# Hybrid attention block: window and selected branch through one exponential, in a trail of four pairs

## The reference, cut to what matters

```
def compressed_attention(q, k, v, slopes):      # 127 blocks of keys, each from 32 positions
    s = q.k * dh ** -0.5 - slopes * dist;  p = masked_softmax(s, mask);  return p.v, p
def select_blocks(p_cmp, T):                    # importance of 64-key blocks, summed over a group
    _, idx = lax.top_k(score, n_sel)            # 16 of 32 blocks for each query
def selected_attention(q, k, v, idx, slopes):   # softmax over the keys of those blocks, dist >= 0
def window_attention(q, k, v, slopes):          # softmax over the last 512 keys
```

## Time and profile before

| | us |
|---|---|
| median of 3 runs (lowest, highest) | 1832.9 (1832.1, 1835.3) |
| profiled execution | 1828.8 |
| its span, slowest core | 1827.8 |
| spans of the 8 cores | 1820.5 to 1827.8 |
| granted TensorE clock, mean | 0.986 to 0.992 |

### The profile page before, as it was taken

One profiled execution on the slowest core, in us unless ns is written; L12 is line 12 of the kernel. 1 busy time (PEld: TensorE's weight loads), 2 busy tenths in 40 slices (PEclk: granted clock), 3 DMA queues, 4 the chain that ended last, 5 costly groups with the idle time before them and its releaser, 6 DMA issues.

```text
span 1827.8 us, 27598 instructions; the slowest of 8 cores (1820.5 to 1827.8 us)
## 1 busy us (share of the span) xinstructions
PE 1714.7 (94%) x9938; PEld 883.2 (48%) x10082; DVE 684.7 (37%) x1257; ACT 502.1 (27%) x834; POOL 81.5 (4%) x157
## 2 busy tenths in 40 slices
PE   4999999999787888998899999999999999999998
PEld 1374746554666663443344444444444444444444
DVE  2334132111676758213635152332415051432415
ACT  4151253232787854445510000000000000000000
POOL 4000000000000010000000000000000000000000
PEclk9999999999999999999999999999999999999999
DMA  9912368334502096525241634527081735436155
GB/s 147 168 17 46 71 115 139 70 63 82 98 2 49 3 200 122 138 50 89 54 85 31 108 59 80 94 45 124 15 138 18 121 48 91 82 57 113 26 93 185
DMA packets 39988, 152.53 MB, mean 83 GB/s; under 512 B 4080, under 2 KB 12848, under 8 KB 26544
## 3 DMA queue, kind: packets, MB, share of 16 engines
q0 software_dynamic: 21456, 126.00, 40.5%
q1 hardware_dynamic: 18400, 24.75, 5.0%
HBM read 265.92 MB, written 8.45 MB: 150 GB/s over the span
## 4 chain that ended last, share of the span: by engine, by line
PE 85%; DMA 4%; DVE 4%; ACT 3%; issue 3%; POOL 0%; DVEq 0%; ACTq 0%; POOLq 0%
PE psum L1252 17%; PE psum L1250 17%; PE psum L1270 16%; PE psum L457 15%; PE psum L1091 6%; PE psum L464 3%; PE psum L900 3%; PE psum L796 3%; DMA arena<-xk 2%; PE psum L1165 2%; PE psum L1216 1%; DMA arena<-wall 1%; ACT arena L903 1%; DMA arena<-memk 1%; PE psum L1052 1%
## 5 line engine op out<-in xcount | busy, mean ns | idle before, releaser
L1078 DVE TENSOR_TENSOR arena<-psum,arena 128x512 f32<-128x512 f32 x432 | 298.3, 691 | 136.9 <-PE psum L1091 64.7
L457 PE MATMUL psum<-arena 128*128 128x512 bf16 (+2 forms) x1600 | 312.4, 354 | 9.7 <-DMA arena<-wall 2.9
L1252 PE MATMUL psum<-arena 128*128 128x512 bf16 x1379 | 316.6, 379 | 1.5
L1250 PE MATMUL psum<-arena 128*128 128x512 bf16 x1379 | 316.4, 379 | 1.5
L1270 PE MATMUL psum<-arena 128*128 128x512 bf16 x1381 | 304.3, 379 | 1.4
L1257 ACT ACTIVATE arena<-psum 128x512 bf16<-128x512 f32 x88 | 52.5, 597 | 824.3 <-PE psum L1250 804.5
L1258 DVE TENSOR_TENSOR arena<-psum,arena 128x512 bf16<-128x512 f32 x88 | 60.9, 692 | 536.2 <-PE psum L1250 423.2
L457 PEld LDWEIGHTS psum<-arena 128*128 128x128 bf16 x1600 | 147.0, 99 | 166.3 <-issue 22.9
L1252 PEld LDWEIGHTS psum<-arena 128*128 128x128 bf16 x1408 | 137.8, 98 | 166.1
L1270 PEld LDWEIGHTS psum<-arena 128*128 128x128 bf16 x1408 | 137.8, 98 | 166.1
L1250 PEld LDWEIGHTS psum<-arena 128*128 128x128 bf16 x1408 | 137.7, 98 | 166.0
(11 more groups left out here) (131 smaller groups left out, 979.4 us busy)
## 6 DMA issues: line engine op xcount, KB each, us to landing
arena<-wall POOLq DMA_DIRECT2D x102, 1024.0 KB, 13.3
arena<-wall POOLq DMA_DIRECT2D x10, 864.0 KB, 11.0
arena<-xk POOLq DMA_DIRECT2D x32, 256.0 KB, 46.3
arena<-xo SPq DMA_DIRECT2D x32, 256.0 KB, 8.1
y<-arena SPq DMA_DIRECT2D x32, 256.0 KB, 2.7
arena<-selscr SPq DMA_DIRECT2D x4, 1024.0 KB, 7.8
arena<-arena SPq DMA_DIRECT2D x16, 144.0 KB, 7.7
arena<-cbf SPq DMA_DIRECT2D x1, 1032.8 KB, 6.9
```

The lines of the kernel that those rows point to most:

```text
L457: op(PE, lambda: nc.tensor.matmul(bank[psi][:, 0:n], lhsT=wt[:, kc, cc * 128:(cc + 1) * 128], rhs=rhs(kc), start=(kc == 0), stop=(kc == 15 ...
L1078: op(DVE, lambda: nc.vector.tensor_tensor(out=dst, in0=bank[psi][:, :], in1=dst, op=ALU.add), r=[bankb[psi]], w=[xrb[d][tc]])
L1250: op(PE, lambda: nc.tensor.matmul(bank[pg][:, :], lhsT=wgt[:, kc, cc * 128:(cc + 1) * 128], rhs=h3T[tc][kc // 4][:, kc % 4, :], start=(kc ...
L1252: op(PE, lambda: nc.tensor.matmul(bank[pu][:, :], lhsT=wut[:, kc, cc * 128:(cc + 1) * 128], rhs=h3T[tc][kc // 4][:, kc % 4, :], start=(kc ...
```

## The change

The diff, cut to what acts. `cmp_job`, `branch_jobs` and the tiles change names in places that are left out.

```diff
-        qnT = self.tile(A, "qnT", [128, NH, TQ], BF16)
+        CT = self.scope()
+        qnT = self.tile(CT, "qnT", [128, NH, TQ], BF16, hi=True)
...
-        NP_ = 8
-        Pt = [self.tile(AT, f"Pt{j}", [128, 512], BF16) for j in range(NP_)]
+        NP_ = 7
+        Pt = [self.tile(AT, f"Pt{j}", [128, 2, 512], BF16) for j in range(NP_)]
-        rot_S = Rot([0, 1, 6])
-        rot_O = Rot([2, 4])
-        rot_T = Rot([7])
-        oc1 = [self.tile(AT, f"oc1_{j}", [128, 4, 128], F32) for j in range(4)]
+        sring = {"p": 0}
+        opair = {"s": 4, "w": 6}
+        def s_pair():
+            p = (sring["p"] + 1) // 2 * 2 % 4
+            sring["p"] = (p + 2) % 4
+            return p
+        def s_one():
+            p = sring["p"]
+            sring["p"] = (p + 1) % 4
+            return p
+        def o_swap():
+            opair["s"], opair["w"] = opair["w"], opair["s"]
+        oc1 = [self.tile(AT, f"oc1_{j}", [128, 4, 128], F32) for j in range(8)]
...
+        M = self.tile(AT, "selM", [128, 16, 512], BF16)     # now behind HG.close()
-        catA = self.tile(CT, "catA", [128, 8, TQ], BF16, hi=True)
+        catA = qnT
+        catTb = qnTb + [[self.buf(f"catT{c}_{t}") for t in range(2)] for c in range(8)]
-        def run_jobs(jobs, L=5):
+        def run_jobs(jobs, L=4, D=2):
+            pjs = []
+            done = 0
+            for n in range(len(jobs) + L + 2):
                 if n < len(jobs):
+                    pjs.append(jobs[n][0]())
+                if 0 <= n - D < len(jobs) and jobs[n - D][2] is not None:
+                    jobs[n - D][2](pjs[n - D])
+                while done < len(jobs) and done <= n - L:
+                    if jobs[done][3] and done == n - L:
+                        break
+                    jobs[done][1](pjs[done])
+                    done += 1
...
+        def stream(g, h, tc, oc, ocbuf, at=None):
             qts = QT[tc * 4:tc * 4 + 4]
+            for dl in range(qts[3] + 1):
                 j0 = min(j for j in range(4) if qts[j] >= dl)
+                last = dl == qts[3]
+                parts = [1, 0] if dl <= 4 else [1]
+                def sc(dl=dl, j0=j0, parts=parts):
+                    si = s_pair() if len(parts) == 2 else s_one()
+                    n0 = j0 * 128
+                    for part in parts:
+                        bi = si + (1 - part if len(parts) == 2 else 0)
...                          # triangle and score matmuls into bank bi, as before
+                    if len(parts) == 2:
+                        src = psum[:, si * 512:(si + 2) * 512].rearrange("p (b n) -> p b n", b=2)[:, :, n0:512]
+                        op(ACT, lambda: nc.scalar.activation(out=Pt[pj][:, :, n0:512], in_=src, func=AF.Exp, bias=ba), r=[bankb[si], bankb[si + 1], pvb], w=[Ptb[pj]])
+                    else:
+                        op(ACT, ...)             # one bank, as before
+                def mask(pj, dl=dl, j0=j0): ...  # the same masks, as a function of their own
+                def pvf(pj, dl=dl, j0=j0, parts=parts, last=last):
+                    if dl == 0:
+                        o_swap()
+                        st["s"], st["w"] = opair["s"], opair["w"]
+                    for part in parts:
+                        b0 = st["s" if part else "w"]
+                        vs = g if part else 2 + g
+                        pv(pj, 1 - part, j0, b0, ..., NV, dl == 0, last if part else dl == 4)
+                    if dl == 4:
+                        finish(st["w"], NV, h, tc, 2, oc, ocbuf, "add" if tc == 1 else "first")
                     if last:
+                        finish(st["s"], NV, h, tc, 1, oc, ocbuf, "last", ocb[cj], ocbb[cj])
-                            later.append([9, outT])
+                        later.append([4, outT])
+                jobs.append((sc, pvf, mask, dl == 0))
+                for f in (at or {}).get(dl, ()):
+                    f()
...
-                later.append([1 + 2 * j, lambda j=j: one(j)])
+                later.append([1 + j, lambda j=j: one(j)])
-            later.append([11, mbuild])
+            later.append([7, mbuild])
...
+        c1(0, True)
+        c1(1, True)
         for g in range(2):
             for hl in range(4):
                 h = 4 * g + hl
                 o_, ob_ = oc0[hl % 2], oc0b[hl % 2]
+                at = {5: [lambda: cmp_job(g, h, 0, o_, ob_)]}
+                if h == 0:
+                    at[6] = [lambda: c1(2)]
+                    at[7] = [lambda: c1(3)]
+                stream(g, h, 0, o_, ob_, at)
             for hl in range(4):
+                h = 4 * g + hl
+                stream(g, h, 1, oc1[h], oc1b[h], {8: [lambda: c1(4 + hl)]} if g == 0 else None)
```

More of the change, by code:

```diff
@@ L790, in acc_view, with pv @@
             return psum[:, b0 * 512:(b0 + 2) * 512].rearrange("p (b n) -> p b n", b=2)[:, :, 0:2 * nv].rearrange("p b (j n) -> p b j n", j=2)
-        def pv(pj, j0, b0, vap, vbufs, nv, first, last):
+        def pv(pj, part, j0, b0, vap, vbufs, nv, first, last):
             for j in range(j0, 4):
@@ L795, in pv @@
                 o0 = (j % 2) * nv
-                op(PE, lambda: nc.tensor.matmul(bank[ob][:, o0:o0 + nv], lhsT=Pt[pj][:, j * 128:(j + 1) * 128], rhs=vap(j), start=(first and j % 2 == 0), stop=last, skip_group_check=True), r=[Ptb[pj]] + vbufs(j), w=[bankb[ob]])
+                op(PE, lambda: nc.tensor.matmul(bank[ob][:, o0:o0 + nv], lhsT=Pt[pj][:, part, j * 128:(j + 1) * 128], rhs=vap(j), start=(first and j % 2 == 0), stop=last, skip_group_check=True), r=[Ptb[pj]] + vbufs(j), w=[bankb[ob]])
         def finish(b0, nv, h, tc, br, oc, ocbuf, mode, dst=None, dstb=None):
@@ L842, in run_jobs @@
                         it[1]()
+            assert done == len(jobs)
             while later:
@@ L858, in sc @@
                 pj = rot_P.next()
[L859 removed]
+                op(ACT, lambda: nc.scalar.activation(out=Pt[pj][:, 0, :], in_=bank[si][:, :], func=AF.Exp), r=[bankb[si]], w=[Ptb[pj]])
                 return pj
             def pvf(pj):
[L863 to L865 removed]
+                if swap:
+                    o_swap()
+                b0 = opair["w"]
+                pv(pj, 0, 0, b0, lambda j: vcaug[:, g, 0:nv], lambda j: [vcaugb], nv, True, True)
+                rj = finish(b0, nv, h, tc, 0, oc, ocbuf, "first" if tc == 1 else "add")
                 if tc == 1:
@@ L911, in sc, with mask @@
+                def mask(pj, dl=dl, j0=j0):
+                    if tc == 1 and dl > 0:
                         md = mdiag(dl, j0)
+                        n0 = j0 * 128
+                        pvw = Pt[pj][:, 0, n0:512]
                         if md is not None:
@@ L939, in branch_jobs, with outT @@
-                jobs.append((sc, pvf))
+                    if dl == 4:
+                        n0 = j0 * 128
+                        pvw = Pt[pj][:, 1, n0:512]
+                        op(DVE, lambda: nc.vector.tensor_tensor(out=pvw, in0=pvw, in1=WIN[:, n0:512], op=ALU.mult), r=[cbb], w=[Ptb[pj]])
+                def pvf(pj, dl=dl, j0=j0, parts=parts, last=last):
+                    if dl == 0:
+                        o_swap()
+                        st["s"], st["w"] = opair["s"], opair["w"]
+                    for part in parts:
+                        b0 = st["s" if part else "w"]
+                        vs = g if part else 2 + g
+                        pv(pj, 1 - part, j0, b0, lambda j: Vaug[:, qts[j] - dl, vs, :], lambda j: [Vaugb[qts[j] - dl]], NV, dl == 0, last if part else dl == 4)
+                    if dl == 4:
+                        finish(st["w"], NV, h, tc, 2, oc, ocbuf, "add" if tc == 1 else "first")
+                    if last:
+                        cj = rot_ocb.next()
+                        finish(st["s"], NV, h, tc, 1, oc, ocbuf, "last", ocb[cj], ocbb[cj])
+                        def outT():
+                            tb2 = s_one()
+                            tv = bank[tb2].bitcast(BF16)
+                            for j in range(4):
+                                op(PE, lambda: nc.tensor.transpose(out=tv[:, j * 128:(j + 1) * 128], in_=ocb[cj][:, j, :], identity=ident), r=[ocbb[cj], cidb], w=[bankb[tb2]])
+                            copy_op(evac_engine(), catA[:, h, tc * 512:(tc + 1) * 512].rearrange("p (f n) -> p f n", f=NPH), tv[:, 0:512].rearrange("p (n f) -> p f n", f=NPH), r=[bankb[tb2]], w=[catTb[h][tc]])
+                        later.append([4, outT])
@@ L982, in build @@
         A.close()
-        self.free([b for l in KnTb for b in l] + Vaugb + [b for l in qnTb for b in l] + [gatesb, kcmpb, vcaugb, cbb])
+        self.free([b for l in KnTb for b in l] + Vaugb + [gatesb, kcmpb, vcaugb, cbb])
         self.mark("conv")
```

90 lines of the change are left out of this document (18 added, 72 removed).

## The result

The changed kernel takes 1851.9 us (median of 4 runs, 1851.4 to 1856.9) against 1832.6 for the kernel before beside it: ratio 1.0112 [1.0099, 1.0124], slower by some 20 us. Forecast was 23 us faster.

What follows compares the result with a forecast made beforehand. Attention was taken as bound by ScalarE in last-512 parts, by no full engine in first-512 parts. Parts of 41, 52, 27, 46 and 3 us give 169 against 192, 23 less: 1832.9 - 23 = 1810 us, range 1800 to 1822.

Steps and rivals of the forecast that it cites:

- The unit price of the exponential: Attention's paired branch exponentials: one over two banks costs 1.01 us, saving 0.15 each, 80 x 0.15 = 12 us of ScalarE.
- Who is the bound of a stream afterwards?: Engine sums per attention stream: first-512 ScalarE 6.3 us, TensorE 5.9, VectorE 5.8; last-512 ScalarE 10.6, VectorE 9.6.
- The coupling charges: Allowance for engines delaying each other: 1.0 us per last-512 stream, 0.5 per first-512 stream, 0.2 in group 0's last-512 streams.
- Moved jobs: Second group's compressed jobs and top-k enter first group's last-512 part, costing VectorE 4 x 2.2 + 5.6 us there.
- Stays hidden: The selection's load has at least three first-512 streams, 20 us, ahead of its first use in either group, so no wait.
- First-512 streams: Attention's first-512 parts: four streams at 6.8 us, 27 per group; parts 41 against 46 and 27 against 45 us.
- With it the half clock stays: At each group's top-k TensorE's stand remains near 4 to 5 us, and the half clock remains; nothing gained.
- Masks two behind: Masks queued two pairs later on VectorE end its 9.1 and 7.8 us stands for ScalarE, so finishes are not held.
- Does it survive?: After attention, the convolution's 23.4 us weight-block wait moves along with attention's end, neither eating nor adding to the 23 us.
- Rival C: Stream starts: TensorE waits 1.35 to 3.5 us for the pair the last finish reads; 1844 at 2.2 us; chance 0.05.
- the output in the queries' place: Attention's output copy: no instruction added, the copy waits for score matmuls four steps back on TensorE; costs nothing.

## Why the prediction was wrong

- **The unit price of the exponential: right.** Forecast 1.01 us, measured 1.01; two instructions instead cost 9 us. The Trainium skill ("VectorE: DVE Perf Modes", TRN2 errata) states 172 cycles plus one per element at 1.2 GHz, from which an estimate is 997 ns; the trace's 1.01 us agrees.
- **"Who is the bound of a stream afterwards?": the step that failed.** I summed each engine over the whole stream, 10.6 for ScalarE and 9.6 for VectorE, and took the larger. The sums themselves were nearly right (VectorE 9.3 busy, ScalarE 11.0; TensorE, which I left out for these streams, 10.0). What failed is that the largest sum, with 1.0 for coupling, was taken for the length. Even without masks a stream takes 11.6 us with ScalarE busy for 10.8. With them the stream runs as two parts with different bounds: five pairs at ScalarE's 1.01, where VectorE has at most one mask per step and stands 3.0, and then the rest, into which VectorE's two finishes and most of its masks have slid: 11.0 of queue. 14.0, not 10.6. The run that took the window's finish out shortened the stretch by 1.5 us and left the stand as it was. The masks' queue accounts for 17 of the 20 us of loss.
- **The coupling charges: mis-sized.** 1.0 us on top of 10.6 per last-512 stream, against a measured 3.0 to 3.6 in group 1 (13.6 to 14.2), 2.0 to 2.6 of it beyond the 11.6 of a stream without masks; 0.2 on top of 11.8 in group 0, against 5.4 and more on core 7. I had written down the danger ("a finish of 1.95 ahead of it can take more than 4 x 0.58 = 2.3 less 0.34") and priced it as if it came now and then; it comes in every stream, twice.
- **"Moved jobs", the compressed ones: priced as VectorE time alone.** Ahead of short jobs (0.25 to 0.36 us each on ScalarE) 2.2 us of queue empties four score banks. Moving them behind the masks gave 7 us back.
- **"Stays hidden", the selection's load: wrong** by up to 2.7 us. Its second half landed at 498.9, 22 us after the first was issued (476.95), and only 16 us of first-512 streams stood behind the issue, not three streams. In the old order the second half's windows of four heads came next, which need no selection mask; in the new one the mask is needed in the first stream's second job.
- **First-512 streams: mis-sized**, 8.6 to 10.2 us against 6.8, masks or no masks. On core 0 of the run without masks attention takes 190.3 us against the forecast 169, and some 15 of these 21 us lie in the first-512 parts. The same step failed, with other engines: TensorE stands for ScalarE in the pairs, then ScalarE for TensorE's saved-up products, 2.4 us against the 0.5 charged. That it is the doubled products of the first job is refuted: without that step these streams stay at 8.6 to 8.8. What else sets their length no run took apart.
- **"With it the half clock stays": wrong**, it doubled or more. Over the eight cores of the profiled run a straight line, with some 2 us of scatter, gives 0.42 us of attention for each further us at 1.2 GHz; over those of the run without masks, where the points lie close to it (188.7 us with 10.9, 196.1 with 28.3), 0.41. So the 24 us more of core 7 go with some 10 of its loss, and the 15 more of the median core with some 6. These are correlations and overlap with the terms above; no run took the clock alone.
- **Masks two behind: right in sign** in the new order (10 us), nothing in the old.
- **"Does it survive?": right** for the slowest core: 1189.9 us behind attention against 1189.1.
- **Rival C, the slower one, was right in sign alone.** Its place, the pair still read by the last finish, is refuted: TensorE waits there 3 times and not 16, and bringing these products one step nearer to it made more such waits and cost 0 us.

What stays open: some 2 us of each last-512 stream that no edit of the order recovered; the some 2 us by which each first-512 stream exceeds its sum; why flushing the products costs as much as 22 us; and the output in the queries' place, which was never tried alone and whose cost of nothing is argued only.

## What to carry to other kernels

Where a row of jobs has phases with different demands, take the largest engine phase by phase, together with the stand in which one engine waits for the other at each turn; the maximum over the whole stream is a lower bound only. Before work is moved or merged, list what will stand ahead of each mask or other small product in its in-order queue, and compare that with the time that the lead banks hold at the length of the jobs there. VectorE's spare time in the busy table was worth little: in the merged order half of each microsecond of masks or finishes that was taken away showed in the total, in the old order a tenth.

## What the runs showed of the hardware

ScalarE reads two neighbouring banks in one instruction at 1.01 us for 128x1024 of float32, back to back, against 0.58 for one bank.

TensorE's clock can fall without a long stand. In the run without masks (core 3) it fell at 576.1 us, in a stretch of paired jobs in which TensorE had only waited 0.3 to 0.6 us per step; the 16 products that came next followed each other every 0.11 us, against some 0.06 at full clock (16 in 1.08 us, at 593.13 above).
```profile
575.34 0.38 PE L918 MATMUL psum<-arena 128*128 128x128 bf16 x4 [0.46 <-ACT arena L923]
576.13 0.37 PE L918 MATMUL psum<-arena 128*128 128x128 bf16 x2 [0.41 <-ACT arena L923]
576.30 1.94 PE L808 MATMUL psum<-arena 128*128 128x129 bf16 x16
```
The stretch around it by windows has a clock of 0.87 with TensorE busy for 81% of it:
```profile
560.00:600.00 40.00, 32.45 (x391) 25.96 (x389) 21.36 (x55) 27.71 (x39) 0.00 (x0) 0.87 0.21 40
```
On core 3 the three first-512 streams in which it fell take 10.1 to 10.3 us; on core 0 of the same run, where it did not fall, 8.6 to 8.9.
